# Head sums of the first block's mixer: transposed squares summed by VectorE, in place of products with two moving columns

## The chip, the cores and the metric

The kernel runs on one core of one Trainium2 chip, as a single launch. The metric is the device time of that launch in microseconds (us), the median of several runs. TensorE (PE in the profile, its weight loads PEld) multiplies; VectorE (DVE), ScalarE (ACT) and GpSimd (POOL) work on what it leaves; SyncE (SP) issues the loads of the weights. All arithmetic is fp32, or fp32 split into two rounded parts.

## The reference

Two blocks of two layers each work on one sequence of 256 tokens and width 1024. A layer is a feed-forward part, a mixer and another feed-forward part. The change touches only the mixer of the first block, which runs twice (once per layer). It projects the normalised input into four branches, each 256 wide, and puts their outputs through `w_out`:

```python
def headwise_rms(x, g, n):          # n = 64 for gla, fox, sc; 128 for ssd
    shp = x.shape
    y = rms_norm(x.reshape(shp[:-1] + (shp[-1] // n, n)), g.reshape(-1, n))
    return y.reshape(shp)
...
qh = rms_norm(q.astype(f32).reshape(Bsz, L, H, D), q_norm) * (D ** -0.5)   # fox: q, and k likewise
```

So six arrays of 256 channels x 256 tokens need, for each token, the sum of squares over each head: fox's queries, fox's keys, and the outputs of ssd, fox, gla and sc. For a head of 64 channels that is 4 sums for each token, for ssd's groups of 128 channels it is 2. The inverse root of each mean then scales the head.

## The kernel before, in words

An array lies with channels on the 128 partitions: `[128, 2 * 256]`, two tiles `t` of channels, each with 256 tokens. Tokens come in two tiles `T` of 128. Sums over channels are sums over partitions, which TensorE does.

The mixer's loop runs over stages `c` (0 to 37), the same on every engine, each engine in its own fixed order. In a stage TensorE first does `chunk(c)`, the products of one slot of weights (up to stage 29, 24 products of 256 columns or so; L604 to L606, L647 to L649), or `acc_slot`, 12 products of 512 columns into the output sums (from stage 30 on; L663 to L665). After that come the small steps of the branches. PSUM has eight banks. The table `AFTER1` says for each stage which small results take which bank; `claim` makes TensorE wait until the bank's last user has been read, `full` reports a result, `drained` reports that a bank was read.

The path of one set of head sums, for example "gla":

- ScalarE squares the branch's output.
- `sums` (L850) takes each of the four 128x128 tiles of squares as the stationary operand and the two columns of `half` as the moving one (`ones[:, 0:2]` for ssd). The tile of results is 128 tokens x 2 heads. The four land side by side in one PSUM bank, 8 columns in all, 16 for queries and keys together. Every one of these products shows as two instructions in the profile.
- VectorE's `inverse_root` (L1616 to L1629) finds the inverse root in a row of small dependent operations on those 8 or 16 columns, in PSUM except for its running result. Its last instruction (L1627, or L1629 for fox) writes the factors spread over 64 or so channels of each head, `[128, 512]`, and reports the sums' bank as drained.
- `spread` (L795) waits for that and turns the factors back with four transposes, so that they multiply the output channel-wise (`scaled`, L1919; `normal`, L1874, for queries and keys).

The order around it on TensorE, by stage: 15 `inputs_turned` (four transposes, L834), sums of the queries' squares; 16 `rows_turned` (two transposes, L842), sums of the keys' squares; 17 `segments((0, 1))`, which starts at L769 by claiming banks 0 and 1, and `state_scores`; 18 the two spreads of queries and keys; 23 ssd's sums, 24 ssd's spread; 25 fox's sums, 26 its spread; 30 gla's sums; 31 gla's spread, then sc's sums; 32 sc's spread; 33 to 37 only products with `w_out`. A whole stage lies between sums and spread everywhere, and VectorE's factors must be ready by then.

VectorE's order: 14 `rows_ended` (L1844 is its end); 17 `steps_applied` (L1851, L1855), then the factors of queries and keys; 18 `gq` (L1982) and `decayed`; 24 ssd's factors; 26 fox's; 31 gla's; 32 `scaled("gla")` (L1919), then sc's factors.

Of the kernel before, what the change touches and what calls it, by code (L numbers as in the profile page):

```python
# [27 lines left out]
ALU = mybir.AluOpType  # L28
ACT = mybir.ActivationFunctionType
AX = mybir.AxisListType.X  # L30

P = 128
SEQ, D, FF, DEPTH = 256, 1024, 2816, 2
# [29 lines left out]
def slot1(c):  # L63
# [4 lines left out]

IP_BANK1 = [6, 5, 4, 7] + [6 - m % 2 for m in range(4, CHUNKS1 // 2)]
SCORED1, TURNED1 = {21: 0, 22: 1}, {22: 0, 23: 1}  # L70
AFTER1 = {9: (("gla_z", 0),), 15: (("xsT", 3), ("qk_sums", 4)), 16: (("rowsT", 2),),
          17: (("seg0", 0), ("seg1", 1), ("sc0", 7)), 18: (("fox_rq", 2), ("fox_rk", 3)), 19: (("seg2", 0), ("seg3", 1), ("sc1", 4)),
          21: (("ssd_y", 7),), 22: (("fox_o0", 4),), 23: (("fox_o1", 0), ("ssd_sums", 7)),
          24: (("gla_kd", 1), ("gla_att0", 2), ("gla_att1", 3), ("ssd_r", 7)), 25: (("fox_sums", 4),), 26: (("fox_r", 4),),
# [207 lines left out]
def build(nc, x_d, w_d, gain_d, last_gain_d, par1_d, par2_d, con_d, out_d):  # L282
    with ExitStack() as ctx:
# [32 lines left out]
        def c_(name):  # L316
            return con[:, CON[name][0]:CON[name][1]]
# [13 lines left out]
        def carve(fields):  # L331
# [13 lines left out]
            ("fqk", 1024), ("fsq", 1024), ("fT", 1024), ("bv", 512), ("xd", 512), ("av", "xd"), ("avs", "lrT"),  # L345
            ("Lm", 1536), ("Mt", 1536), ("P", "Lm"), ("pt", "Mt"), ("kdT", "xbcs"), ("attT", "fqk"), ("states", "rows"), ("Y", "gates"),
            ("sq", "fsq"), ("dc", "fT"), ("dy", "Lm"),
            ("dt", 8), ("nm", 8), ("rowsum", 8), ("rl", 8), ("rf", 16), ("ralogx", 1)])
        M2_ = carve([
            ("kx", 1024), ("blk", 960), ("kr", 512), ("qraw", 1024), ("qr", 1024), ("mr", 2048),  # L350
            ("vsw", 512), ("mv", 1024), ("gate", 64), ("gex", SEQ), ("hidT", 512), ("hid", 128),
# [4 lines left out]
        def m1(name, width):  # L356
            return mix[:, M1_[name]:M1_[name] + width]
# [31 lines left out]
        def wait_full(eng, L, name):  # L389

            b, _, _, by_slot = L.turns.of[name]
            if by_slot is None:
                eng.wait_ge(bank_full[b], L.fulls(name) + 1)
            else:
                eng.wait_ge(slot_used, L.slot0 + (by_slot + 1 + RING))

        def wait_drained(eng, L, name):

            b, k = L.bank(name)
            eng.wait_ge(bank_read[b], k + 2)  # L400

        def claim(pe, L, name):

            b, k = L.bank(name)
            pe.wait_ge(bank_read[b], k + 1)
            return bank[b]
# [28 lines left out]
        def psum(L, name):  # L435
            return bank[L.bank(name)[0]]

        def full(L, name, ins):
            ins.then_inc(bank_full[L.bank(name)[0]], 1)

        def drained(L, name, ins):
            ins.then_inc(bank_read[L.bank(name)[0]], 1)
# [146 lines left out]
        def _(pe):  # L589
# [215 lines left out]
            def first_mixer(L):  # L805
# [36 lines left out]
                        mm = pe.transpose(out[:, T * P:(T + 1) * P], m1("rsp", SEQ)[:, T * P:(T + 1) * P], ident)  # L842
                    full(L, "rowsT", mm)

                def sums(out, squares, at, groups):

                    for T in range(NT):
                        for t in range(2):
                            c = at + T * 4 + t * 2
                            mm = pe.matmul(out[:, c:c + 2], squares[:, t * SEQ + T * P:t * SEQ + (T + 1) * P], groups, start=(T == 0 and t == 0 and at == 0),  # L850
                                           stop=True, skip_group_check=True)
                    return mm

                def segments(heads):

# [70 lines left out]

                def branch_sums(b):

                    out = claim(pe, L, f"{b}_sums")
                    pe.wait_ge(ev(f"{b}_squares"), L.l * (2 if b == "fox" else 1) + (2 if b == "fox" else 1))  # L930
                    c = (b in ("fox", "sc")) * 512
                    full(L, f"{b}_sums", sums(out, m1("sq", 1024)[:, c:c + 512], 0, ones[:, 0:2] if b == "ssd" else c_("half")))

                def branch_spread(b):

                    out = claim(pe, L, f"{b}_r")
                    wait_drained(pe, L, f"{b}_sums")
                    full(L, f"{b}_r", spread(out, factors_of(b)))

                def keys_turned():  # L940
# [61 lines left out]
                for c in range(2, STAGES1):  # L1002
                    if c in SCORED1:
                        pair_scores(SCORED1[c])
                    if c in TURNED1:
                        turn_probs(L, TURNED1[c], m1("P", 1536)[:, TURNED1[c] * 768:(TURNED1[c] + 1) * 768])
                    if c == 27:
                        gla_states_wait()
                    if c < CHUNKS1:
                        if c != NO_SLOT:  # L1010
                            chunk(c)
                    else:
                        i, t = (c - CHUNKS1) // 2, (c - CHUNKS1) % 2
                        if c < STAGES1 - 2:
                            if t == 0:
                                wait_drained(pe, L, f"{BRANCHES[i]}_r")
                            acc_slot(L, FFN_SLOTS + slot1(c), sources[i][:, t, :], rests[i][:, t, :], wo, c == CHUNKS1)
                        elif c == STAGES1 - 2:
                            made = lambda: wait_drained(pe, L, "sc_r")
                            tail(L, [(FFN_SLOTS + slot1(c) + t, sources[3][:, t, :], rests[3][:, t, :], made) for t in range(2)], wo, (L, 2))  # L1020
                    if c == 9:
                        gate_logits()
                    if c == 15:
                        inputs_turned()
                        out = claim(pe, L, "qk_sums")
                        pe.wait_ge(ev("qk_squares"), L.l * 2 + 1)
                        sums(out, m1("fsq", 1024)[:, 0:512], 0, c_("half"))
                    if c == 16:
                        rows_turned()
                        pe.wait_ge(ev("qk_squares"), L.l * 2 + 2)  # L1030
                        full(L, "qk_sums", sums(psum(L, "qk_sums"), m1("fsq", 1024)[:, 512:1024], 8, c_("half")))
                    if c == 17:
                        segments((0, 1))
                        state_scores(0)
                    if c == 18:
                        for i, name in enumerate(("fox_rq", "fox_rk")):
                            out = claim(pe, L, name)
                            wait_drained(pe, L, "qk_sums")
                            full(L, name, spread(out, factors_of("qk")[:, i * 512:(i + 1) * 512]))
                    if c == 19:  # L1040
                        segments((2, 3))
                        state_scores(1)
                    if c == 21:
                        state_outputs()
                    if c in (22, 23):
                        pair_weighted(c - 22)
                    if c == 23:
                        branch_sums("ssd")
                    if c == 24:
                        keys_turned()  # L1050
                        gla_scores()
                        branch_spread("ssd")
                    if c == 25:
                        branch_sums("fox")
                    if c == 26:
                        branch_spread("fox")
                    if c == 27:
                        gla_states()
                    if c == 29:
                        gla_outputs()  # L1060
                    if c == 30:
                        branch_sums("gla")
                    if c == 31:
                        branch_spread("gla")
                        branch_sums("sc")
                    if c == 32:
                        branch_spread("sc")
# [541 lines left out]
        def _(dve):  # L1609
            def inverse_root(own, wide, sums, n, count, after=None):  # L1610

                v, vh, t = (sums[:, c:c + n] for c in (32, 64, 96))
                out = m1("rf", 16)[:, 0:n]
                spread_out = wide.rearrange("p (g n) -> p g n", n=HD)
                each = lambda ap: ap.unsqueeze(2).to_broadcast([P, n, HD])
                own.step(dve.tensor_scalar(v, sums[:, 0:n], 1.0 / count, EPS, ALU.mult, ALU.add))  # L1616
                own.step(dve.tensor_scalar(vh, sums[:, 0:n], -0.5 / count, -0.5 * EPS, ALU.mult, ALU.add))
                own.wait()
# [148 lines left out]
            def first_mixer(L, own):  # L1767
# [127 lines left out]
                def pair_kept(t):  # L1895

                    for e in range(2):
                        wait_full(dve, L, ("pt", t, e))
                        c = (2 * t + e) * 384
                        drained(L, ("pt", t, e), dve.tensor_copy(m1("pt", 1536)[:, c:c + 384], psum(L, ("pt", t, e))[:, 0:384]))  # L1900

                def factors(b):

                    name = f"{b}_sums"
                    wait_full(dve, L, name)
                    sums = psum(L, name)
                    if b == "fox":
                        for step in range(2):
                            own.link(dve.tensor_tensor(sums[:, 0:8], sums[:, 0:8], rl, ALU.mult))
                    ins = inverse_root(own, factors_of(b), sums, 8, P if b == "ssd" else HD, after=rl if b == "fox" else None)  # L1910
                    drained(L, name, ins)

                def scaled(b):

# [45 lines left out]
                for c in range(STAGES1):  # L1960
# [11 lines left out]
                    if c == 14:  # L1972
                        rows_ended()
                    if c == 17:
                        steps_applied()
                        wait_full(dve, L, "qk_sums")
                        ins = inverse_root(own, factors_of("qk"), psum(L, "qk_sums"), 16, HD)
                        drained(L, "qk_sums", ins)
                    if c == 18:
                        dve.wait_ge(ev("gla_exp"), L.one)  # L1980
                        wait_full(dve, L, ("ip", GQ))
# [489 lines left out]
```

## Time and profile before

| what | value |
|---|---|
| median of 3 runs | 2069.29 us (2068.7 to 2070.6) |
| the profiled execution: its own time | 2066.66 us |
| the profiled execution: span, first to last instruction | 2064.9 us |
| PE busy | 2038.2 us, 99% of the span |
| DVE busy | 802.8 us, 39% |
| ACT busy | 1083.1 us, 52% |
| POOL busy | 1576.1 us, 76% |
| PE's share of the chain that ended last | 96% |

Busy times of PE are modelled for pipelined products: two of them overlap, so that the start of the next one tells more than the length of the first. The chain that ended last gives each piece of time to one instruction; in it, PE's pieces are counted from when the instruction could follow the last one, about 0.16 us later than the starts in the timeline. The first mixer's stages 15 to 32 lie at about 245 to 323 us of the span in the first layer and at about 759 to 837 us in the second.

### The profile page before, as it was taken

The page shows a single profiled execution, that of the slowest core. Times are in us where ns is not written, and L with a number is a line of the kernel's source. Part 1 is how long each engine was busy: PE and PEld are TensorE (multiplying, and loading weights), DVE is VectorE, ACT ScalarE, POOL GpSimd, SP SyncE. Part 2 cuts the span into 40 slices and gives each one's busy share as a digit, 9 for nine tenths or more (in the row PEclk, how much of TensorE's full clock was granted, in tenths as well). Part 3 has the DMA queues.
Part 4 walks back from the last instruction along what each step waited for, and adds up shares of the span by engine and source line. Part 5 has one row for each costly group of instructions (what it writes and reads, how often), then busy time and mean ns, then how long its engine had stood idle before and what let it go on. Part 6 is the DMA issues. An engine that isn't in the chain of part 4 may idle for free.

```text
span 2064.9 us, 35135 instructions
## 1 busy us (share of the span) xinstructions
PE 2038.2 (99%) x12228; PEld 1760.4 (85%) x12228; DVE 802.8 (39%) x1789; ACT 1083.1 (52%) x1875; POOL 1576.1 (76%) x667
## 2 busy tenths in 40 slices
PE   8999999999999999999999999999999999999998
PEld 7888988888888898888888888788888889878886
DVE  3223744222422374422232247632233225663223
ACT  5445545444544554544454458654455446755443
POOL 6888756888888874688888876478887887556886
PEclk9999999999999999999999999999999999999999
DMA  7555534555555553355555554455555555454553
GB/s 252 189 186 183 184 113 133 193 186 191 178 189 183 177 183 122 134 191 185 185 182 183 191 190 143 166 161 189 187 191 175 183 189 181 143 184 155 187 188 112
DMA packets 101122, 362.30 MB, mean 175 GB/s; under 512 B 11824, under 2 KB 12976, under 8 KB 100912
## 3 DMA queue, kind: packets, MB, share of 16 engines
q1 hardware_dynamic: 100320, 359.45, 52.0%
q10 hardware_dynamic: 720, 1.74, 0.2%
q8 instruction: 53, 0.87, 0.2%
q14 instruction: 29, 0.24, 0.0%
HBM read 360.10 MB, written 1.05 MB: 175 GB/s over the span
## 4 chain that ended last, share of the span: by engine, by line
PE 96%; DVE 2%; DMA 1%; ACT 1%; issue 0%; SPq 0%; DVEq 0%; ACTq 0%
PE twin L602 31%; PE twin L606 20%; PE twin L663 9%; PE twin L665 9%; PE twin L664 9%; PE twin L604 5%; PE twin L605 5%; PE twin L779 1%; PE twin L647 1%; PE twin L722 1%; PE twin L648 1%; PE twin L649 1%; DMA raw<-in_w_dram 1%; PE twin L785 1%; PE twin L1112 1%; PE twin L1109 1%
## 5 line engine op out<-in xcount | busy, mean ns | idle before, releaser
L568 POOL TENSOR_TENSOR wlo<-raw,whi 128x1024 fp32r<-128x1024 f32 x663 | 1575.9, 2407 | 473.2 <-ACT whi L1275 473.1
L1275 ACT CAST whi<-raw 128x1024 fp32r<-128x1024 f32 x664 | 677.2, 1051 | 73.4 <-PE twin L606 35.5
L606 PE MATMUL twin<-turned,wlo 128*128 128x256 f32 x1952 | 549.8, 282 | 0.0
L602 PE MATMUL twin<-turned,whi 128*128 128x512 f32 x1344 | 480.5, 400 | 1.6 <-DVE turned L1659 1.6
L602 PE MATMUL twin<-early,whi 128*128 128x512 f32 x1344 | 479.9, 398 | 0.5
L606 PE MATMUL twin<-early,wlo 128*128 128x256 f32 x1536 | 431.2, 281 | 0.0
L1719 DVE TENSOR_TENSOR twin<-twin,mix 128x512 f32<-128x512 f32 x168 | 117.5, 699 | 758.0 <-ACT mix L1334 758.0
L606 PEld LDWEIGHTS twin<-turned,wlo 128*128 128x128 f32 x1952 | 370.9, 190 | 3.3
L1334 ACT COPY mix<-twin 128x512 f32<-128x512 f32 x168 | 98.5, 586 | 439.3 <-PE twin L606 439.3
L602 PEld LDWEIGHTS twin<-turned,whi 128*128 128x128 f32 x1344 | 253.0, 188 | 64.5 <-DVE turned L1659 1.6
L602 PEld LDWEIGHTS twin<-early,whi 128*128 128x128 f32 x1344 | 252.4, 188 | 64.1 <-issue 2.0
L606 PEld LDWEIGHTS twin<-early,wlo 128*128 128x128 f32 x1536 | 290.3, 189 | 3.4
L663 PE MATMUL twin<-whi,hhi 128*128 128x512 f32 x720 | 283.6, 394 | 0.0
L665 PE MATMUL twin<-wlo,hhi 128*128 128x512 f32 x720 | 283.6, 394 | 0.0
L664 PE MATMUL twin<-whi,hlo 128*128 128x512 f32 x720 | 281.3, 391 | 0.0
L1340 ACT ACTIVATE mix<-twin 128x256 f32<-128x256 f32 x176 | 67.7, 385 | 254.6 <-DVE twin L1725 254.6
L604 PE MATMUL twin<-turned,whi 128*128 128x256 f32 x608 | 175.7, 289 | 0.1
L605 PE MATMUL twin<-turned,whi 128*128 128x256 f32 x608 | 171.9, 283 | 0.0
L663 PEld LDWEIGHTS twin<-whi,hhi 128*128 128x128 f32 x720 | 135.3, 188 | 32.3 <-DVE hlo L1729 3.0
L665 PEld LDWEIGHTS twin<-wlo,hhi 128*128 128x128 f32 x720 | 135.1, 188 | 30.0
L664 PEld LDWEIGHTS twin<-whi,hlo 128*128 128x128 f32 x720 | 135.3, 188 | 23.5
L1725 DVE TENSOR_TENSOR twin<-twin,root 128x512 f32<-128x512 f32 x176 | 123.1, 699 | 24.0 <-PE twin L606 12.7
(287 smaller groups left out, 2081.8 us busy)
## 6 DMA issues: line engine op xcount, KB each, us to landing
raw<-in_w_dram SPq DMA_DIRECT2D x680, 512.0 KB, 3.3
con<-in_con_dram ACTq DMA_DIRECT2D x1, 1113.5 KB, 7.3
x<-in_x_dram SPq DMA_DIRECT2D x2, 256.0 KB, 4.4
x<-in_x_dram SPq DMA_DIRECT2D x1, 512.0 KB, 6.2
mix<-in_last_gain_dram SPq DMA_DIRECT2D x1, 512.0 KB, 4.3
out_dram<-xs SPq DMA_DIRECT2D x2, 256.0 KB, 2.9
out_dram<-xs ACTq DMA_DIRECT2D x2, 256.0 KB, 3.3
par<-in_par_dram SPq DMA_DIRECT2D x2, 208.0 KB, 3.9
```

The costliest lines, as they stand in the source:

```text
L568: nc.gpsimd.tensor_tensor(wlo[:, place, :], raw[:, place, :], whi[:, place, :].bitcast(F32), ALU.subtract).then_inc(split_done, 1)
L602: pe.matmul(out, hi, both.rearrange("p c n -> p (c n)"), start=start and k == 0, stop=False, skip_group_check=True)
L604: pe.matmul(out[:, 0:SEQ], hi, both[:, 0, :], start=start and k == 0, stop=False, skip_group_check=True)
L605: pe.matmul(out[:, 0:SEQ], hi, both[:, 1, :], start=False, stop=False, skip_group_check=True)
L606: mm = pe.matmul(out[:, 0:SEQ], lo, both[:, 0, :], start=False, stop=stop and k == KD - 1, skip_group_check=True)
L663: pe.matmul(o, ahi[:, T * P:(T + 1) * P], hi, start=first, stop=False)
L664: pe.matmul(o, alo[:, T * P:(T + 1) * P], hi, start=False, stop=False)
L665: mm = pe.matmul(o, ahi[:, T * P:(T + 1) * P], lo, start=False, stop=last)
L1275: nc.scalar.copy(whi[:, place, :], raw[:, place, :]).then_inc(hi_done, 1)
L1334: nc.scalar.copy(kept[:, s], tiles[s][:, :, SEQ:2 * SEQ]).then_inc(lower_done, 1)
L1719: dve.tensor_tensor(both, both, kept[:, s], ALU.add).then_inc(summed, 1)
L1725: dve.tensor_tensor(both, both, root[:].unsqueeze(1).to_broadcast([P, 2, SEQ]), ALU.mult).then_inc(rooted_done, 1)
```

## The change

`sums` no longer multiplies. It transposes the four tiles of squares into a bank, 512 columns, with tokens on the partitions. VectorE sums each head's 64 (ssd: 128) columns with one `tensor_reduce` into `sums`, a new small field in SBUF, and frees the bank. `inverse_root` works wholly in SBUF, on the widened field `rf`. It reports the factors by a semaphore of their own (`{b}_factors`, `qk_factors`), on which `spread` waits. ssd gets 4 columns in place of 8. The queries' and the keys' squares no longer fit one bank together: `q_sums` takes bank 4 as `qk_sums` did, and `k_sums` takes bank 1, ahead of `seg1`. VectorE sums the queries' squares at the start of its stage 17 and the keys' after `steps_applied`.

```diff
-AFTER1 = {9: (("gla_z", 0),), 15: (("xsT", 3), ("qk_sums", 4)), 16: (("rowsT", 2),),
+AFTER1 = {9: (("gla_z", 0),), 15: (("xsT", 3), ("q_sums", 4)), 16: (("rowsT", 2), ("k_sums", 1)),
           17: (("seg0", 0), ("seg1", 1), ("sc0", 7)), ...
...
-            ("dt", 8), ("nm", 8), ("rowsum", 8), ("rl", 8), ("rf", 16), ("ralogx", 1)])
+            ("dt", 8), ("nm", 8), ("rowsum", 8), ("rl", 8), ("sums", 16), ("rf", 64), ("ralogx", 1)])
...
-                def sums(out, squares, at, groups):
+                def sums(name, squares):
 
+                    out = claim(pe, L, name)
                     for T in range(NT):
                         for t in range(2):
-                            c = at + T * 4 + t * 2
-                            mm = pe.matmul(out[:, c:c + 2], squares[:, t * SEQ + T * P:t * SEQ + (T + 1) * P], groups, start=(T == 0 and t == 0 and at == 0),
-                                           stop=True, skip_group_check=True)
-                    return mm
+                            c = T * SEQ + t * P
+                            mm = pe.transpose(out[:, c:c + P], squares[:, t * SEQ + T * P:t * SEQ + (T + 1) * P], ident)
+                    full(L, name, mm)
...
                 def branch_spread(b):
 
                     out = claim(pe, L, f"{b}_r")
-                    wait_drained(pe, L, f"{b}_sums")
+                    pe.wait_ge(ev(f"{b}_factors"), L.one)
                     full(L, f"{b}_r", spread(out, factors_of(b)))
...
             def inverse_root(own, wide, sums, n, count, after=None):
 
-                v, vh, t = (sums[:, c:c + n] for c in (32, 64, 96))
-                out = m1("rf", 16)[:, 0:n]
+                v, vh, t, out = (m1("rf", 64)[:, c:c + n] for c in (0, 16, 32, 48))
...
+                def summed_squares(name, sums):
+
+                    wait_full(dve, L, name)
+                    n = sums.shape[1]
+                    drained(L, name, dve.tensor_reduce(sums, psum(L, name)[:].rearrange("p (g n) -> p g n", g=n), AX, ALU.add))
+                    wait_drained(dve, L, name)
+
                 def factors(b):
 
-                    name = f"{b}_sums"
-                    wait_full(dve, L, name)
-                    sums = psum(L, name)
+                    n = 4 if b == "ssd" else 8
+                    sums = m1("sums", 16)[:, 0:n]
+                    summed_squares(f"{b}_sums", sums)
                     if b == "fox":
                         for step in range(2):
-                            own.link(dve.tensor_tensor(sums[:, 0:8], sums[:, 0:8], rl, ALU.mult))
-                    ins = inverse_root(own, factors_of(b), sums, 8, P if b == "ssd" else HD, after=rl if b == "fox" else None)
-                    drained(L, name, ins)
+                            own.link(dve.tensor_tensor(sums, sums, rl, ALU.mult))
+                    inverse_root(own, factors_of(b), sums, n, P if b == "ssd" else HD, after=rl if b == "fox" else None).then_inc(ev(f"{b}_factors"), 1)
...
                     if c == 17:
+                        summed_squares("q_sums", m1("sums", 16)[:, 0:8])
                         steps_applied()
-                        wait_full(dve, L, "qk_sums")
-                        ins = inverse_root(own, factors_of("qk"), psum(L, "qk_sums"), 16, HD)
-                        drained(L, "qk_sums", ins)
+                        summed_squares("k_sums", m1("sums", 16)[:, 8:16])
+                        inverse_root(own, factors_of("qk"), m1("sums", 16), 16, HD).then_inc(ev("qk_factors"), 1)
```

## Rows read from the trace of the kernel before

**Rows 1.** The page: busy time by engine; granted clock in 40 slices.
```profile
PE 2038.2 (99%) x12228; PEld 1760.4 (85%) x12228; DVE 802.8 (39%) x1789; ACT 1083.1 (52%) x1875; POOL 1576.1 (76%) x667
...
PEclk9999999999999999999999999999999999999999
```

**Rows 2.** Waits of PE, whole span: who for whom, us in total, times, longest.
```profile
PE twin L795 <- DVE mix L1629: 1.7, 2, 0.9
...
PE twin L795 <- DVE mix L1627: 1.5, 4, 0.4
```

**Rows 3.** The chain that ended last, 245 to 259 us: start, us, what.
```profile
245.25 0.44 PE twin L834 x4
245.69 0.79 PE twin L850 x8
246.48 0.23 PE twin L604
...
258.26 0.87 PE twin L795 x8
```

**Rows 4.** The same chain, 284 to 291 us (ssd).
```profile
284.38 0.98 PE twin L850 x8
...
289.87 0.59 PE twin L795 x4
290.46 0.12 PE twin L604
```

**Rows 5.** Timeline of DVE, 249 to 256 us: start, us, instruction.
```profile
250.89 0.16 DVE L1851 COPY mix<-twin 128x8 f32<-128x8 f32 x1
251.16 0.69 DVE L1855 TENSOR_TENSOR mix<-twin,mix 128x512 f32<-128x512 f32 x1
251.76 0.17 DVE L1616 TENSOR_SCALAR twin<-twin 128x16 f32<-128x16 f32 x1
...
254.19 1.22 DVE L1627 SCALAR_TENSOR_TENSOR mix<-twin,mix 128x1024 f32<-128x1024 f32 x1
```

**Rows 6.** Timeline of PE: the first products of `segments`.
```profile
253.29 0.40 PE L769 MATMUL twin<-maskT,identR 128*128 128x256 f32 x2
```

**Rows 7.** The chain again, 297 to 299 us: from fox's factors to its spread.
```profile
297.83 0.14 issue
297.96 0.63 PE twin L795 x4
298.59 0.26 PE twin L604
```

**Rows 8.** Timelines of PE (four rows) and DVE (two), 313 to 323 us.
```profile
313.56 0.95 PE L850 MATMUL twin<-con,mix 128*128 128x2 f32 x8
...
317.73 0.63 PE L795 MATMUL twin<-con,mix 128*128 128x128 f32 x4 [0.34 <-DVE mix L1627]
...
318.19 0.95 PE L850 MATMUL twin<-con,mix 128*128 128x2 f32 x8
...
322.44 0.63 PE L795 MATMUL twin<-con,mix 128*128 128x128 f32 x4 [0.39 <-DVE mix L1627]
...
319.26 0.17 DVE L1616 TENSOR_SCALAR twin<-twin 128x8 f32<-128x8 f32 x1
...
322.21 0.68 DVE L1928 TENSOR_TENSOR early<-twin,early 128x512 fp32r<-128x512 f32 x1
```

**Rows 9.** DVE's groups by form: reductions; busy us, mean ns, idle before.
```profile
L1893 DVE TENSOR_REDUCE mix<-twin 128x2 f32<-128x512 f32 x4 | 2.7, 681 | 0.0
```

**Rows 10.** The same view: small operations that write PSUM or SBUF.
```profile
L1646 DVE TENSOR_TENSOR twin<-twin,stat 128x2 f32<-128x2 f32 x36 | 6.1, 168 | 1.2
...
L2276 DVE TENSOR_TENSOR stat<-stat 128x2 f32<-128x2 f32 x3 | 0.5, 162 | 0.1
```

**Rows 11.** Stretches: us, busy PE, PEld, DVE, ACT, POOL, then granted clock.
```profile
5.00:10.00 5.00, 2.17 (x9) 1.83 (x10) 2.47 (x5) 3.09 (x6) 0.00 (x0) 1.00 0.90 275
10.00:15.00 5.00, 5.00 (x24) 4.27 (x24) 0.90 (x4) 4.01 (x10) 3.55 (x2) 1.00 1.02 410
```

More of the change, by code:

```diff
@@ L927, in branch_sums @@
                 def branch_sums(b):
-                    out = claim(pe, L, f"{b}_sums")
                     pe.wait_ge(ev(f"{b}_squares"), L.l * (2 if b == "fox" else 1) + (2 if b == "fox" else 1))
                     c = (b in ("fox", "sc")) * 512
-                    full(L, f"{b}_sums", sums(out, m1("sq", 1024)[:, c:c + 512], 0, ones[:, 0:2] if b == "ssd" else c_("half")))
+                    sums(f"{b}_sums", m1("sq", 1024)[:, c:c + 512])
                 def branch_spread(b):
                     out = claim(pe, L, f"{b}_r")
-                    wait_drained(pe, L, f"{b}_sums")
+                    pe.wait_ge(ev(f"{b}_factors"), L.one)
                     full(L, f"{b}_r", spread(out, factors_of(b)))
@@ L1024, in first_mixer @@
                         inputs_turned()
-                        out = claim(pe, L, "qk_sums")
                         pe.wait_ge(ev("qk_squares"), L.l * 2 + 1)
-                        sums(out, m1("fsq", 1024)[:, 0:512], 0, c_("half"))
+                        sums("q_sums", m1("fsq", 1024)[:, 0:512])
                     if c == 16:
@@ L1030, in first_mixer @@
                         pe.wait_ge(ev("qk_squares"), L.l * 2 + 2)
-                        full(L, "qk_sums", sums(psum(L, "qk_sums"), m1("fsq", 1024)[:, 512:1024], 8, c_("half")))
+                        sums("k_sums", m1("fsq", 1024)[:, 512:1024])
                     if c == 17:
@@ L1037, in first_mixer @@
                             out = claim(pe, L, name)
-                            wait_drained(pe, L, "qk_sums")
+                            pe.wait_ge(ev("qk_factors"), L.one)
                             full(L, name, spread(out, factors_of("qk")[:, i * 512:(i + 1) * 512]))
@@ L1610, in inverse_root @@
             def inverse_root(own, wide, sums, n, count, after=None):
-                v, vh, t = (sums[:, c:c + n] for c in (32, 64, 96))
-                out = m1("rf", 16)[:, 0:n]
-                spread_out = wide.rearrange("p (g n) -> p g n", n=HD)
-                each = lambda ap: ap.unsqueeze(2).to_broadcast([P, n, HD])
+                v, vh, t, out = (m1("rf", 64)[:, c:c + n] for c in (0, 16, 32, 48))
+                spread_out = wide.rearrange("p (g n) -> p g n", n=count)
+                each = lambda ap: ap.unsqueeze(2).to_broadcast([P, n, count])
                 own.step(dve.tensor_scalar(v, sums[:, 0:n], 1.0 / count, EPS, ALU.mult, ALU.add))
```

## The prediction, made blind

> **What bounds the kernel.** I read the page first: PE is busy for 99% of the span and the granted clock is at its top in all slices [rows 1]. So the time is PE's, and what counts is either PE work that goes away or time in which PE waits. The second view was the waits of PE. Apart from the start and the second block it waits only at L795, the spreads, for the last instruction of VectorE's factor chain: twice for fox (L1629) and four times for gla and sc (L1627) [rows 2]. Nowhere does it wait for weights in the first mixer. The reader should see that three of the six sets of sums (fox, gla, sc) already sit on the path sums, factors, spread, and that the other three (queries, keys, ssd) are hidden behind a stage of products. The third view was the chain in order of time, for prices on PE, and the fourth the timeline of DVE, for what is queued there. The two layers' mixers show the same pattern 514 us apart, so I work out one and double it.
>
> **PE work removed.** Eight short products take 0.79 us, and the next product then takes 0.23 in place of 0.12; four transposes with other short products behind them cost 0.44, eight in a row 0.87 [rows 3]; four alone cost 0.59, with 0.12 for the product after them [rows 4]. So:
> - Queries: 0.44 + 0.79 + 0.23 = 1.46 becomes eight transposes, 0.87 + 0.12 = 0.99: -0.47.
> - Keys: two transposes, half of 0.44, and 0.79 + 0.23 make 1.24; it becomes six transposes, halfway between 0.59 and 0.87, so 0.73 + 0.12: -0.39.
> - ssd: 0.98 + 0.23 = 1.21 [rows 4] becomes 0.59 + 0.12 = 0.71: -0.50; where the extra 0.19 of its start stays, -0.31. I take -0.40.
> - fox, gla, sc: -0.3 to -0.5 each of PE work, but PE waits there, so this shortens nothing by itself; what counts is when the last of the sums is done, 0.79 - 0.44 = 0.35 earlier.
>
> With nothing else that would be about 2.2 us per layer, 4.4 in all.
>
> **VectorE work added.** One reduction of 128x512 from PSUM: the nearest row, a maximum with 2 outputs in place of a sum with 4 or 8, is 0.681 us [rows 9]. The wait behind it is at most the 0.11 between the end of L1851 and L1855, which wait for the same kind of report (251.05 to 251.16) [rows 5], and not under nothing; I take 0.04, so 0.72 in all. The inverse root's operations move from PSUM to SBUF. A small operation that writes PSUM takes 168 ns, one all in SBUF 162 [rows 10]; some ten write PSUM today, so I credit 0.07 per chain. The last, wide instruction stays as it is.
>
> Here a page speaks for a larger credit. VectorE: DVE Perf Modes, in its section on the SBUF errata of the Trainium skill, gives an operation from PSUM 120 cycles of fixed cost and one in SBUF 58. By that, 13 links would save 62 cycles at 0.96 GHz each, an estimate of 0.84 us per chain, more than the reduction costs. The trace disagrees: 168 against 162 ns for the same operation and width [rows 10]. I go by the trace.
>
> **Queries and keys: a new wait.** This is the step that I think decides the first half. PE reaches `segments` at 253.29 now [rows 6]; with -0.47 and -0.39 it would be there at 252.43. But `segments` first claims bank 1, which now holds the keys' squares until VectorE has summed them. VectorE is the late one: it is free for stage 17 at 250.89 [rows 5]. From there: the queries' reduction 0.72, so L1851 at 251.61; L1851 and L1855 keep their pitch (250.89 to 251.76 is 0.87), so the keys' reduction starts at 252.48 and ends at 253.16. PE follows a VectorE release by 0.14 [rows 7], so `segments` starts at 253.30: the whole 0.86 is given back as a wait. A group behind a wait also costs more: 0.63 + 0.26 [rows 7] against 0.59 + 0.12 [rows 4] for four transposes, 0.18. Products with other operands may restart cheaper; I take +0.10 in all for queries and keys, bounds 0 and +0.25. Queued behind PE's wait are `segments` and `state_scores`, and behind them ScalarE's exponentials, which start when they do now.
>
> The factors then begin at 253.20, 1.44 later than 251.76, and the spread wants them at 258.10 (the chain's 258.26 [rows 3] less 0.16, by which it runs behind the timeline): the wide L1627 starts 2.43 after the chain (254.19 - 251.76) and takes 1.22 [rows 5], so they are there at 253.20 + 2.36 + 1.22 + 0.14 = 256.92. That is 1.2 us of cover; without it every further delay on VectorE would be PE's. `gq` and `decayed` shift by about 1.4 us and still end before `normal` is due.
>
> **ssd.** The factors shift by 0.72 - 0.35 - 0.07 against the sums, +0.30. From sums to a waiting spread the chain takes 4.17 today (gla's 317.73 - 313.56 [rows 8]), so ssd's factors would be there for PE at 284.38 + 0.19 + 4.17 = 288.74, and the spread starts at 289.87 [rows 4]. With the change 289.04 stands against 289.47: 0.4 us of cover are left, nothing waits, and -0.40 stays as a gain. Without the cover it would cost what the chain is late.
>
> **fox, gla, sc.** Here PE's next start is set by VectorE.
> - fox: from the start of the sums to the spread +0.72 - 0.35 - 0.07 = +0.30.
> - gla: the same, +0.30 on 317.73 - 313.56 = 4.17 [rows 8].
> - sc: VectorE does `scaled("gla")` ahead of sc's factors. It begins sc's chain at 319.26, when that ends, while sc's sums are already there (their 0.95 end at 319.14). So earlier sums buy nothing, and it pays the reduction in full: +0.72 - 0.07 = +0.65 between the two spreads, 4.71 today [rows 8].
>
> After sc's spread only products with `w_out` follow. For gla, L1928 ends at 322.89, right behind sc's factors [rows 8]; TensorE wants its result only in stage 34, a whole slot of 12 products after sc's spread, and sc's own in stage 36. That cover holds, and the shift stays to the end of the kernel: PE has no other slack to soak it up in.
>
> **The sum.** Per layer: +0.10 - 0.40 + 0.30 + 0.30 + 0.65 = +0.95; for two layers +1.9 us. The profiled execution took 2066.66 us by its own clock (span 2064.9 and 1.8 around it), so a like one would take 2068.6. The three runs lie higher, at a median of 2069.29; against them the forecast is 2071.2. Bounds per layer: low 0 - 0.50 + 0.25 + 0.25 + 0.58 = +0.58, high +0.25 - 0.31 + 0.40 + 0.40 + 0.75 = +1.49, so +1.2 to +3.0. A change of 0.2% is 4.1 us, about what a measurement of this kernel can tell from no change. So: no difference that can be told, on the slower side of nothing.
>
> **Rivals.**
> - A, the bank is no obstacle. If the keys' squares are summed before PE asks, queries and keys give -0.86 in place of +0.10: two layers -0.02, time 2069.3. For it: VectorE is only 0.87 late. Against it: L1844 to L1855 are dependent work with no gap [rows 5]. Chance 0.12.
> - B, the chain in SBUF gets so short that it pays for the reduction: 0.72 over 13 links, 55 ns off each of 168. Then fox and gla go to -0.35 each and sc to 0, a layer to +0.10 - 0.40 - 0.70 = -1.00, in all -2.0: 2067.3, still within the bound. Together with A it is -3.9: 2065.4, and a little more would be faster. 162 ns against 168 speaks against it [rows 10]. Chance 0.03 alone, 0.02 with A.
> - B is what the page on VectorE named above makes of it; its 0.84 per chain would put the sum at 2066.6.
> - C, slower: the clock. PE's waits grow; before sc's spread 0.39 [rows 8] becomes about 1.5 us, and twelve sets of transposes stand where products stood. If the granted clock fell from 2.4 to 1.2 GHz for just one slot behind each sc spread, its 12 products, which take at most 3.1 us today (a slot's worth lies between the end of sc's sums, 318.19 + 0.79, and the wait that ends at 322.44 [rows 8]), would take as much again, in all 6.2, with the sum 2077.4. It decides from the first slot per layer that shows a lower clock. The trace speaks against it: the clock stayed at 1.00 in 10 to 15 us, right after 5 us in which PE worked 2.17, and though eight transposes (of the input) lie in both stretches [rows 11]. Chance 0.03.
> - C's rule is also on a page: TensorE: Matmul & The Clock Gate, Part 4, in the Trainium skill, says that transposes do not count as activity in the way that products do. In the stretches just named no such loss is seen.
> - D, the costs of waiting pile up: several terms at or past their high bounds, +4.2 and more. Chance 0.05.
>
> **How the numbers follow.** My case, all that lies between +1.2 and +3.0 and what measurement adds, has 0.75. Slower by over 0.2%: C and D, 0.08. Faster by over 0.2%: 0.03, for A with B and for what I have not seen. The rest, 0.89, is within. The range for 8 in 10 is the sum's own, 2070.5 to 2072.3, widened by the spread of the runs (about 1 us to either side) and down towards A: 2068.4 to 2073.8.
>
> **What the next profile would show.** L850's products are gone, 48 transposes stand there at 0.44 to 0.59 us per four, and PE's work falls by some 4 us. A new wait of 0.8 to 0.9 us at L769's line stands behind VectorE's reduction, twice. The reductions take 0.68. The small operations take near 165 ns. The waits at the spreads grow from 0.9 and 0.4 to about 1.5 for fox, 1.2 for gla and 1.6 for sc, and ssd's spread doesn't wait. The sum fails if the new wait isn't there (A), if the small operations are clearly under 160 ns (B), if a clock under 1.00 shows between 240 and 340 us (C), or if ssd's or the queries' spread waits.

## The result, and the profile after

The changed kernel takes 2096.57 us (median of 4 runs, 2096.16 to 2098.05) against 2068.99 us: 1.0139 times as long, 95% interval 1.0127 to 1.0151. That is 27.6 us more, where 1.9 us more was forecast, and far outside the range of 2068.4 to 2073.8. In the experiments below one execution of e1 (2834.58 us) and one of e2 (3345.45 us) ran at a granted clock of 0.655 and 0.555 and are left out of their figures.

The page of the changed kernel, its span and the busy times:

```profile
span 2095.0 us, 35010 instructions
...
PE 2039.9 (97%) x12180; PEld 1762.1 (84%) x12180; DVE 836.0 (40%) x1801; ACT 1084.9 (52%) x1875; POOL 1576.7 (75%) x667
```

PE is as busy as before [rows 1] but only for 97% of a span that is 30 us longer (the profiled execution of before was one of its quicker ones). So the time is mostly waiting. The waits of PE, changed kernel (us in all, times, longest); L1624 and L1626 are what L1627 and L1629 were:

```profile
PE twin L795 <- DVE mix L1624: 19.2, 6, 7.5
PE twin L795 <- DVE mix L1626: 11.7, 2, 5.8
...
PE twin L769 <- issue: 1.5, 2, 0.8
```

Beside [rows 2], the waits at the spreads grew from 3.2 to 30.9 us, and ssd's spread is now among them. The third row is the wait for bank 1 that was forecast, 0.8 us, twice. It starts PE's segments when the prediction said, at 253.30 (timeline of PE, changed kernel; the second row is fox's spread, at 297.96 before [rows 7]):

```profile
253.30 0.47 PE L769 MATMUL twin<-maskT,identR 128*128 128x256 f32 x2 [0.77 <-issue]
...
303.71 1.09 PE L795 MATMUL twin<-con,mix 128*128 128x128 f32 x4 [5.85 <-DVE mix L1626]
```

Why fox's factors are so late stands in the timelines of DVE and of POOL, same kernel:

```profile
295.03 0.69 DVE L1903 TENSOR_REDUCE mix<-twin 128x8 f32<-128x512 f32 x1 [2.13 <-PE twin L851]
...
296.64 0.17 DVE L1617 TENSOR_SCALAR mix<-mix 128x8 int32<-128x8 int32 x1
296.85 2.23 DVE L1619 TENSOR_TENSOR mix<-mix 128x8 f32<-128x8 f32 x1
299.11 2.32 DVE L1620 TENSOR_TENSOR mix<-mix 128x8 f32<-128x8 f32 x1
301.47 0.17 DVE L1622 SCALAR_TENSOR_TENSOR mix<-mix 128x8 f32<-128x8 f32 x1
301.67 0.17 DVE L1619 TENSOR_TENSOR mix<-mix 128x8 f32<-128x8 f32 x1
```

```profile
296.69 4.72 POOL L568 TENSOR_TENSOR wlo<-raw,whi 128x1024 fp32r<-128x1024 f32 x2 [3.54 <-ACT whi L1273]
```

In gla's chain it is first a `tensor_scalar`, an operation with one SBUF input, that is held to the end of a split (same two timelines):

```profile
322.57 2.38 DVE L1614 TENSOR_SCALAR mix<-mix 128x8 f32<-128x8 f32 x1
```

```profile
320.12 4.80 POOL L568 TENSOR_TENSOR wlo<-raw,whi 128x1024 fp32r<-128x1024 f32 x2 [3.42 <-ACT whi L1273]
```

The reader should see that the same instruction on 8 columns takes 0.17 or 2.3 us, and that the slow ones end with GpSimd's splits (a split is its subtraction over the 1024 columns of a weight slot, 2.4 us). For fox, two splits run from 296.69 to 301.41; L1619 begins just behind the start of the first and ends at 299.08, L1620 begins at 299.11 and ends at 301.43. In the first layer's ssd chain one operation is held so, in fox's two, in gla's three, in sc's and in that of queries and keys none; the second layer repeats it (its waits are 9.7 and 5.8 us, the first's 9.6 and 5.8).

The long waits have an echo. Stretches of the changed kernel; after the busy times of PE, PEld, DVE, ACT and POOL stands the granted clock:

```profile
300.00:305.00 5.00, 1.29 (x6) 1.32 (x7) 4.06 (x11) 0.00 (x0) 1.41 (x1) 0.63 0.84 285
305.00:310.00 5.00, 5.00 (x49) 4.80 (x47) 0.72 (x2) 1.53 (x2) 2.37 (x1) 0.69 0.08 31
```

The clock fell to its lower level, 1.2 GHz, while PE stood still for 5.85 us, and stayed there for part of both stretches. In the chain, 16 products behind the spread take 0.21 us in place of 0.12, and from fox's spread to the next small step (303.71 to 309.09) PE needs 5.4 us, before 3.6 (297.96 to 301.54).

### The profile page after: what moved, and what is told of

Its sections match the earlier page's. It is cut to its first block, busy times and chain, and to the rows that moved or that the text cites. A ratio compares the mean times of both kernels' runs of the same rounds, so it can differ in the third digit from the quotient of the medians.

```text
span 2095.0 us, 35010 instructions
## 1 busy us (share of the span) xinstructions
PE 2039.9 (97%) x12180; PEld 1762.1 (84%) x12180; DVE 836.0 (40%) x1801; ACT 1084.9 (52%) x1875; POOL 1576.7 (75%) x667
## 4 chain that ended last, share of the span: by engine, by line
PE 95%; DVE 3%; ACT 1%; issue 1%; DMA 1%; SPq 0%; DVEq 0%; ACTq 0%
PE twin L602 30%; PE twin L606 20%; PE twin L663 9%; PE twin L665 9%; PE twin L664 9%; PE twin L604 5%; PE twin L605 4%; PE twin L722 1%; PE twin L779 1%; PE twin L647 1%; PE twin L648 1%; PE twin L649 1%; PE twin L785 1%; DVE mix L1620 1%; DVE mix L1619 1%
## 5 line engine op out<-in xcount | busy, mean ns | idle before, releaser
L1722 DVE TENSOR_TENSOR twin<-twin,root 128x512 f32<-128x512 f32 x176 | 123.1, 699 | 23.9 <-PE twin L606 12.7
```

Of the source, the lines that this page charges most:

```text
L1722: dve.tensor_tensor(both, both, root[:].unsqueeze(1).to_broadcast([P, 2, SEQ]), ALU.mult).then_inc(rooted_done, 1)
```

## Experiments

**The theories.** Theory 1: VectorE and GpSimd exclude each other where VectorE's instruction takes all its inputs from SBUF; moving the inverse root's scratch from PSUM to SBUF exposed its chain to GpSimd's 2.4 us splits. Theory 2: the transposes and reductions are what costs. Theory 3: tiny dependent operations in SBUF are slow at times whatever GpSimd does. In the code cuts below, `...` stands for lines left out.

**e1, the scratch back in PSUM.** From the changed kernel:

```diff
-                v, vh, t, out = (m1("rf", 64)[:, c:c + n] for c in (0, 16, 32, 48))
+                v, vh, t = (scratch[:, c:c + n] for c in (32, 64, 96))
+                out = m1("rf", 64)[:, 0:n]
...
```

`scratch` is the bank of the sums, for queries and keys that of the queries; it is drained by the last instruction of the root, on which the spread waits, as before.

> The changed kernel, with one thing put back: the inverse root's scratch (v, vh, t) lies in the PSUM bank of the sums again, only its running result and the sums are in SBUF, so that every two-input operation but the two with the row sums of fox reads one input from PSUM. Transposes, reductions and the keys' squares in bank 1 stay. Theory 1 (VectorE's operations with all inputs in SBUF are held while GpSimd's split of 2.4 us runs): the operations of 2.2 to 2.4 us vanish from the chain, the spreads wait 1 to 2 us each as the prediction had it, and the time is that of the prediction's sum, 2069.5 to 2073. Fox's two multiplications by the row sums may still be held, 2.4 us at most per layer. Theory 2 (the transposes and reductions cost it, as work or as late banks): the time stays at 2090 or more. Theory 3 (tiny dependent operations in SBUF are slow at times whatever GpSimd does): time as in theory 1, so this run does not tell 1 from 3.

Measured: 1.0008 times the kernel before, 0.9999 to 1.0018 (2069.0 against 2067.59 us). The waits of PE in it:

```profile
PE twin L795 <- DVE mix L1625: 5.4, 4, 1.6
PE twin L795 <- DVE mix L1627: 3.3, 2, 1.7
...
PE twin L769 <- issue: 1.5, 2, 0.8
```

The first row counts four waits again and not six: ssd's spread doesn't wait. All 48 transposes and all reductions are in this kernel, and 26 of the 27.6 us are gone. Theory 2 falls. PE is busy for 2033.5 us, 4.7 less than before [rows 1], where 4 less was forecast. The new wait at the segments stays, as it should.

**e2, only the scratch moved.** From the kernel before, nothing but

```diff
-                v, vh, t = (sums[:, c:c + n] for c in (32, 64, 96))
-                out = m1("rf", 16)[:, 0:n]
+                v, vh, t, out = (m1("rf", 64)[:, c:c + n] for c in (0, 16, 32, 48))
```

> The kernel before, with only the inverse root's scratch moved to SBUF; no transposes, no reductions, products with two columns as before. Theory 1: the first two operations still read PSUM, the rest is all in SBUF and is held where GpSimd runs; 20 to 30 us slower, 2089 to 2099. Theory 2: no difference, 2068.5 to 2070. Theory 3: as theory 1.

Measured: 1.0166, 1.0145 to 1.0186 (2099.8 us, the middle of three): this edit alone costs as much as the whole change (the two intervals overlap), a little above what was expected. DVE's groups by form (busy us, mean ns):

```profile
L1624 DVE SCALAR_TENSOR_TENSOR mix<-mix 128x8 f32<-128x8 f32 x16 | 15.5, 968 | 0.5
...
L1619 DVE TENSOR_SCALAR mix<-mix 128x8 int32<-128x8 int32 x8 | 5.7, 717 | 0.3
...
L1616 DVE TENSOR_SCALAR mix<-twin 128x8 f32<-128x8 f32 x8 | 1.2, 156 | 0.0
```

The two forms shown that read only SBUF have means of 1.0 and 0.7 us, the one that reads PSUM is at 156 ns though it writes SBUF. That points to the inputs and not the output, which e5 takes up.

**e3, GpSimd nearly idle.** The changed kernel, scratch in SBUF, with the split of the first block's mixer slots cut to 8 of 1024 columns (the kernel leaves out the lower parts of the other columns):

```diff
...
-                nc.gpsimd.tensor_tensor(wlo[:, place, :], raw[:, place, :], whi[:, place, :].bitcast(F32), ALU.subtract).then_inc(split_done, 1)
+                nc.gpsimd.tensor_tensor(wlo[:, place, 0:8], raw[:, place, 0:8], whi[:, place, 0:8].bitcast(F32), ALU.subtract).then_inc(split_done, 1)
...
```

> The changed kernel; in the first block's mixer GpSimd splits only 8 of the 1024 columns of each slot (the lower parts of the rest are left as they are, so the low products there work on other numbers), which makes its instruction short instead of 2.4 us. Theory 1: no small VectorE operation over 0.3 us in the mixer, time 2069 to 2073. Theory 2 and theory 3: operations of 2.2 us stay, and the time stays above 2090.

Measured: 1.0004, 0.9994 to 1.0014 (2068.44 us). One of DVE's groups and GpSimd's short form:

```profile
L1622 DVE TENSOR_TENSOR mix<-mix 128x8 f32<-128x8 f32 x18 | 3.0, 167 | 0.6
```

```profile
L569 POOL TENSOR_TENSOR wlo<-raw,whi 128x8 fp32r<-128x8 f32 x74 | 15.6, 211 | 237.9 <-ACT whi L1276 237.9
```

VectorE's instructions are those of the changed kernel, and in the first mixer not one is slow. Theory 3 falls. The waits at the spreads are within 0.1 us of e1's (5.3 and 3.3 us in all).

**e4b, GpSimd only writes.** As e3, but the mixer's lower parts are filled with zeros, so that GpSimd reads nothing and the kernel leaves out all of them:

```diff
+                    nc.gpsimd.memset(wlo[:, place, :].bitcast(F32), 0.0).then_inc(split_done, 1)
```

> The changed kernel; in the first block's mixer GpSimd writes zeros over each slot's lower part in place of the split (so the low products there add nothing), which reads nothing from SBUF. If what holds VectorE is a GpSimd instruction that reads SBUF, the chain's operations stay at 0.17 us and the time is 2067 to 2070. If any GpSimd instruction holds them, single operations last as long as the rest of GpSimd's instruction, and the time lies between 2073 and 2097 according to its length.

Measured: 1.0022, 1.0011 to 1.0034 (2072.88 us), between the two cases. The groups say why; GpSimd's instruction takes 0.954 us here:

```profile
L1622 DVE TENSOR_TENSOR mix<-mix 128x8 f32<-128x8 f32 x18 | 3.0, 167 | 0.6
...
L1620 DVE TENSOR_SCALAR mix<-mix 128x8 int32<-128x8 int32 x6 | 2.7, 449 | 0.2
L1616 DVE TENSOR_SCALAR mix<-mix 128x8 f32<-128x8 f32 x6 | 2.6, 439 | 0.2
...
L1617 DVE TENSOR_SCALAR mix<-mix 128x8 f32<-128x8 f32 x6 | 2.5, 412 | 0.0
```

The expectation treated all forms alike and was wrong there. In this run operations with two SBUF inputs are not held by a GpSimd instruction that only writes, though several begin inside one; tensor_scalars from SBUF to SBUF are (singles of 0.9 to 1.0 us).

**e5, form by form.** The kernel before, with this in VectorE's idle time in stage 34, on 8 columns (`ps` in PSUM, the rest in SBUF):

```diff
...
+                        for i in range(5):
+                            own.link(dve.tensor_tensor(pc, pa, pb, ALU.mult))
+                            own.link(dve.tensor_tensor(pc, ps, pb, ALU.mult))
+                            own.link(dve.reciprocal(pc, pa))
+                            own.link(dve.tensor_scalar(pc, pa, 1.0, 1.0, ALU.mult, ALU.add))
+                            own.link(dve.tensor_copy(pc, pd))
+                            own.link(dve.tensor_tensor(ps, pa, pb, ALU.mult))
```

> The kernel before, with 30 extra operations of 8 columns on VectorE behind sc's remainders in stage 34, where it idles for 8 us and GpSimd is busy; nothing else depends on them. Five rounds of six forms: product of two SBUF inputs; of a PSUM and an SBUF input; reciprocal from SBUF; tensor_scalar from SBUF to SBUF; copy from SBUF to SBUF; product of two SBUF inputs into PSUM. Theory 1, in the form that what counts is which inputs lie in SBUF: both products of two SBUF inputs show single operations of up to 2.4 us, whatever they write; the one with a PSUM input and the reciprocal never pass 0.2 us. Tensor_scalar and copy decide whether a single SBUF input is enough: the slow tensor_scalars of the changed kernel say yes. Theory 3 (tiny dependent operations in SBUF as such) has them all slow at times, and not only while GpSimd runs.

One execution, 2078.1 us. Timeline of DVE, from the second form of the diff to the first of its next round, and of POOL:

```profile
327.45 0.17 DVE L2056 TENSOR_TENSOR mix<-twin,mix 128x8 f32<-128x8 f32 x1
327.65 0.20 DVE L2057 RECIPROCAL mix<-mix 128x8 f32<-128x8 f32 x1
327.88 1.99 DVE L2058 TENSOR_SCALAR mix<-mix 128x8 f32<-128x8 f32 x1
329.91 0.17 DVE L2059 COPY mix<-mix 128x8 f32<-128x8 f32 x1
330.11 0.18 DVE L2060 TENSOR_TENSOR twin<-mix 128x8 f32<-128x8 f32 x1
330.32 2.34 DVE L2055 TENSOR_TENSOR mix<-mix 128x8 f32<-128x8 f32 x1
```

```profile
327.44 2.40 POOL L570 TENSOR_TENSOR wlo<-raw,whi 128x1024 fp32r<-128x1024 f32 x1 [1.37 <-ACT whi L1277]
330.24 2.39 POOL L570 TENSOR_TENSOR wlo<-raw,whi 128x1024 fp32r<-128x1024 f32 x1 [0.40 <-ACT whi L1277]
```

Inside the first split the product with a PSUM input and the reciprocal pass in 0.17 and 0.20 us, and the tensor_scalar is held to its end (329.87 against 329.84). The product of two SBUF inputs that begins in the second is held to its end too. The second layer shows the same. The copy and the product into PSUM never began inside a split, so for these two the run says nothing. Theory 1 is too wide as it stands: the reciprocal's only input lies in SBUF, and it passes.

The extra operations did not stay within the idle time, as the expectation had it. PE waited for VectorE behind them, once per layer, and the clock was lower in the stretch that follows (waits of PE, and the stretch behind the first one):

```profile
PE twin L724 <- DVE x L1672: 8.0, 2, 4.0
```

```profile
340.00:345.00 5.00, 5.00 (x22) 4.41 (x23) 2.92 (x6) 2.89 (x8) 0.00 (x0) 0.70 0.00 0
```

**e8, GpSimd in shorter pieces.** The changed kernel, each split cut into four of 256 columns:

```diff
+                for q in range(4):
+                    cols = slice(q * 256, (q + 1) * 256)
+                    ins = nc.gpsimd.tensor_tensor(wlo[:, place, cols], raw[:, place, cols], whi[:, place, cols].bitcast(F32), ALU.subtract)
...
```

> The changed kernel, with each of GpSimd's splits of 1024 columns cut into four of 256, in all of the kernel. Theory 1 has an operation held for the rest of one GpSimd instruction: the longest small operation falls from 2.4 to about 0.6 or 0.7 us, and the chains lose less, 2070 to 2085. If VectorE had to wait for a whole run of GpSimd work and not for one instruction, the 2.4 us stay. A risk: GpSimd gets slower by its start-up costs, and PE then waits for splits in the feed-forward parts.

Measured: 1.0262, 1.0232 to 1.0292 (2122.17 us): a miss. The waits of PE and GpSimd's group:

```profile
PE twin L798 <- DVE mix L1627: 20.9, 7, 6.7
PE twin L798 <- DVE mix L1629: 10.9, 2, 5.4
PE twin L666 <- POOL wlo L570: 10.0, 12, 1.1
```

```profile
L570 POOL TENSOR_TENSOR wlo<-raw,whi 128x256 fp32r<-128x256 f32 x2652 | 1851.7, 756 | 252.9 <-ACT whi L1276 252.8
```

A held product now takes 0.65 us, as expected, but after each one GpSimd begins its next piece, and VectorE gets one operation in between two: eight operations of fox's chain are held in place of two, and the spreads still wait 31.8 us. And a quarter of a split takes 0.756 us, four of them 3.02 in place of 2.4, so the stated risk came true and PE waits for splits.

**e6, the keys' squares first.** e1, with VectorE's order in stage 17 turned round:

```diff
-                        steps_applied()
                         summed_squares("k_sums", m1("sums", 16)[:, 8:16])
+                        steps_applied()
```

> The run with the scratch in PSUM, and VectorE sums the keys' squares before steps_applied in place of behind it. By the prediction's step on bank 1 the keys' reduction then ends at 250.9 + 0.72 + 0.68 = 252.3 and PE may pass at 252.44, when it arrives at 252.4: the wait of 0.8 us at segments goes, 0.9 us per layer. Against the run with the scratch in PSUM 1.5 to 2 us less, which makes 0.9995 to 1.0002 of the kernel before. If segments was never the limit (something else is late behind it), nothing changes: 1.0008.

Measured: 0.9995, 0.9986 to 1.0004 (2067.04 against 2067.90 us). PE's wait at the segments is no longer among its waits. The two ratios differ by 0.0013, 2.7 us, with intervals that overlap. The traces tell more: from the start of the queries' sums to the start of the segments PE needs 7.75 us in e1 and 6.87 in e6, in the first layer, which is the 0.9 us expected.

**e7, only where a stage hides it.** e6, with fox, gla and sc back on products with two columns:

```diff
-                    sums(f"{b}_sums", m1("sq", 1024)[:, c:c + 512])
+                    (sums if b == "ssd" else product_sums)(f"{b}_sums", m1("sq", 1024)[:, c:c + 512])
...
```

> As the run with the keys first, but only queries, keys and ssd, whose factors are hidden behind a stage, are transposed and reduced; fox, gla and sc get their sums by products with two columns as before. By the prediction's terms this keeps -0.86 and -0.4 per layer and drops +0.30, +0.30 and +0.65: -2.5 us in all, 0.9985 to 0.9992 of the kernel before. If the gains on PE are not real, 1.000.

Measured: 0.9983, 0.9974 to 0.9992 (2064.34 us), a little better than expected, and the fastest of all: faster than the kernel before by 3.6 us and than the changed one by 32. In the traces, from the start of the queries' sums to sc's spread, it is 1.34 us faster than before in each layer (75.57 us against 76.91), 2.7 in all, where 2.5 was expected. Its waits at the spreads are those of before [rows 2] again:

```profile
PE twin L795 <- DVE mix L1637: 1.7, 2, 0.9
PE twin L795 <- DVE mix L1635: 1.4, 4, 0.4
```

## Why the prediction was wrong

**The step that failed** is in "VectorE work added": "The inverse root's operations move from PSUM to SBUF. A small operation that writes PSUM takes 168 ns, one all in SBUF 162 [rows 10]; ... so I credit 0.07 per chain." The term is not -0.07 but, per layer, +2.05 for ssd, +4.2 for fox and +6.4 for gla, the excess of the held operations over 0.17 us. e2 shows that this edit alone costs 1.66%, e1 that without it the rest of the change costs 0.08%, e3 that the same instructions are all short when GpSimd is nearly idle.

The row was read rightly and taken from the wrong place. All three L2276 of the kernel before lie at 2057.7 to 2058.8 us, behind GpSimd's last split. The stretch of the kernel before in which it stands (POOL's busy time is the fifth after the length):

```profile
2050.00:2064.90 14.90, 5.47 (x24) 4.13 (x22) 8.28 (x23) 4.23 (x10) 0.00 (x0) 0.75 0.20 71
```

In the mixer GpSimd works for more than half of the time. And the trace of before did hold the warning: of the second block's small operations on 4 columns, the two-input one in SBUF has a mean three times its minimum, the reciprocal next to it has not. Both, kernel before, DVE's groups by form:

```profile
L2081 DVE TENSOR_TENSOR mix<-mix 128x4 f32<-128x4 f32 x16 | 8.3, 518 | 0.6
...
L2079 DVE RECIPROCAL mix<-mix 128x4 f32<-128x4 f32 x16 | 2.8, 176 | 14.6 <-ACT mix L1506 14.6
```

A mean of 518 ns over 16 (165 to 1264) would have shown that the price is not a single one. None of the rivals held this mechanism: D let the costs of waiting pile up, but to +4.2 us and more, where +27.6 was measured. Nor did the last, wide instruction of the chain stay as it was: it now has only SBUF inputs too (`mix<-mix`). In the changed kernel it was never held, at 0.69 us; in e8 one took 1.17.

The Trainium skill has the rule: SBUF — State Buffer, "SBUF: two separate sides", says that VectorE and GpSimd share one pair of ports under an exclusive lock for a whole instruction, that VectorE needs it in its two-port modes and for two SBUF inputs, and for the latter only against a GpSimd operation that reads SBUF. The runs agree in each point that they touch: 2.34 us for the product of two SBUF inputs behind a split of 2.39, 167 ns beside a memset, 0.4 us on average for the tensor_scalars beside the same memset. That these tensor_scalars run in a two-port mode is not shown by any trace.

**The other steps**, each against e1, which has all of the change but the failed term (starts in PE's timeline; before, then e1):
- The credit of 0.07 per chain is not in e1, whose scratch lies in PSUM. e3 has it where nothing is held: from sums to spread fox takes 5.11 us (e1 5.14), gla 4.52 (4.53), and between the spreads sc takes 5.38 (5.43). So it was small where GpSimd is silent, too: 0.01 to 0.05. Without it the forecast for e1 is +0.37, +0.37 and +0.72 for fox, gla and sc.
- Queries and keys, +0.10: segments begin at 253.29 and 253.29, the spread at 258.10 and 258.17, so +0.07. The new wait was right in place, cause and size, and e6 took it away by the order on VectorE alone, as the reason given demands.
- ssd, -0.40: fox's sums begin at 293.17 and 292.74; less the 0.07 that is -0.50, the bound for a start without the extra 0.19.
- fox, +0.37 from sums to spread: 4.79 and 5.14 (292.74 to 297.88), +0.35.
- gla, +0.37: 4.17 and 4.53 (313.49 to 318.02), +0.36.
- sc, +0.72 between the spreads: 4.71 and 5.43 (318.02 to 323.45), +0.72.
- The prediction's reading that PE waits nowhere else in the first block left out one wait of 0.3 us per layer at L722, behind the mixer; no term uses it.
- Together +1.0 per layer, where the forecast without the credit has +1.16; the difference is ssd's 0.10 and small ones. The spans are 2064.9 and 2066.8, +1.9, the medians +1.4. So for the change without the failed term each step came out within 0.1 us, and that +1.9 is also the prediction's sum to the digit is luck: the missing credit and ssd's larger gain cancel.

**In the changed kernel**, first layer: the held operations of 12.7 us, of which ssd's cover takes some 0.4 us, the terms above with +1.0, and what the clock costs. For fox that last is 5.4 - 3.6 = 1.8 us, behind gla about 0.4 (5.85 between the spreads where e1 has 5.43). The sum is 15.5; sc's spread begins 15.45 later than before (337.89 against 322.44). Twice that is 30.9, and the spans differ by 30.1; where the 0.8 went was not traced.

**Rival C** named the clock, but as a loss by itself behind a wait of 1.5 us; e1 waits that long (1.67 us at most) and its clock is 0.998. In the changed kernel's mixers it fell only in the waits of 5.85 and 7.5 us, so there it is a result of the failed term and no cause of its own. The row that the prediction held against C is weak, though. It shows a granted clock of 1.02 from 10 to 15 us [rows 11], but until about 13.5 us PE's products followed each other more slowly. Timeline of PE, kernel before:

```profile
10.98 0.41 PE L606 MATMUL twin<-turned,wlo 128*128 128x256 f32 x1
11.19 0.63 PE L602 MATMUL twin<-turned,whi 128*128 128x512 f32 x1
...
14.48 0.27 PE L606 MATMUL twin<-turned,wlo 128*128 128x256 f32 x1
14.60 0.40 PE L602 MATMUL twin<-turned,whi 128*128 128x512 f32 x1
```

Behind the product of 256 columns the next one starts 0.21 us later at first, as in the changed kernel at the lower level, and 0.12 us later at 14.48. So the recorded clock of that stretch is no evidence against C; e1 is.

**Rival A** (bank 1 no obstacle) was wrong, 0.77 us of wait. **Rival B** (a faster chain in SBUF) was wrong: the chain became longer, and even where nothing holds them (e3) the two-input operations take 167 ns against 174 with a PSUM output at the same width, 7 ns less each where B needed 55. The Trainium skill, VectorE: DVE Perf Modes, "The TRN2 errata", puts the fixed cost of an operation from PSUM 62 cycles above that of one in SBUF. No run here bears that out.

## What to carry to other kernels

Price an operation from rows that stand beside the same neighbours as the place it goes to, and look at its shortest and longest times and not at the mean alone: a row from the end of a kernel, where GpSimd is silent, says nothing of a stretch where GpSimd works. Scratch of a dependent chain on VectorE is better off with one input in PSUM than all in SBUF, as long as GpSimd has long instructions that read SBUF. And put work on the engine that is late only where a whole stage hides it: the same transposes and reductions gain 1.3 to 1.8 us per layer for queries, keys and ssd (e7 against before, by the traces and by the medians), and lose 1.3 to 1.5 for fox, gla and sc (e6 against e7, by the medians and by the traces).

## What the runs showed of the hardware that I had not expected

- One 8-column operation of VectorE takes 0.17 us or up to 2.4 us according to whether a GpSimd split of 2.4 us is under way. Held are products of two SBUF inputs (2.34 us) and tensor_scalars from SBUF to SBUF (L1614 of the changed kernel, in gla's chain, 2.38); not held are one input in PSUM (0.17) and the reciprocal from SBUF (0.20).
- Beside a GpSimd memset of 0.95 us the two-input products are not held (167 ns mean over 18), the tensor_scalars are (0.41 to 0.45 mean over 6, 1.01 at most).
- Cutting GpSimd's instruction into four does not help the chain: 31.8 us of waits at the spreads against 30.9. Each operation that meets the row of pieces is held for one of them, and the four pieces take 3.02 us in place of 2.4.
- PE's granted clock stayed at its upper level through waits of 1.7 us (e1, 0.998 in all) and fell in waits of 4.0 us (e5, 0.70 in the 5 us from 340 on), 5.85 and 7.5 us (changed kernel, 16 products at the slower pace behind the first of these).
